# Where a hybrid attention and mLSTM block splits its output weights and squashes its first two gate tiles

## The reference, cut to what matters

```
u    = rmsnorm(x, pre_norm_w)
proj = u @ w_in                                   # 9 groups of 512 columns and 8 gate columns
y_sb = head_rmsnorm(stick_breaking_attention(q, k, v)) * silu(sb_z)      # 8 heads x 64
y_ml = sigmoid(ml_o) * mlstm(conv(q), conv(k), v, i, f)                  # 4 heads x 128
y_ml = head_rmsnorm(y_ml, ml_norm_w) * silu(ml_z)
h    = x + rmsnorm(concat(y_sb, y_ml) @ w_out, post_norm_w)
out  = h + sigmoid(h @ ple_w_gate + b) * (p @ ple_w_up)
```

## Time and profile before

| what | value |
|---|---|
| median of 3 runs | 1822.59 us (1821.94 to 1824.18) |
| the profiled execution | 1821.69 us |
| its span in the trace | 1819.9 us |
| PE busy in the span | 1767.5 us (97%) |
| ACT, DVE, POOL busy | 999.3, 1129.5, 683.6 us |
| end of the attention's last `b_late` | 1257.7 us |
| start of the mLSTM block | 1277.2 us |
| start of the first output projection | 1313.1 us |

### The profile page before, as it was taken

How to read it: one execution, slowest core, us unless ns; L and a number is a source line. 1 busy time by engine, 2 the same in 40 slices (tenths; PEclk the granted TensorE clock), 3 DMA queues, 4 the chain that set the end, 5 groups by cost and what they waited for, 6 DMA issues and landing times. The chain is left out here.

```text
span 1819.9 us, 28179 instructions
## 1 busy us (share of the span) xinstructions
PE 1767.5 (97%) x8972; PEld 1443.2 (79%) x8972; DVE 1129.5 (62%) x1776; ACT 999.3 (55%) x2045; POOL 683.6 (38%) x946
## 2 busy tenths in 40 slices
PE   7999999999899999999999999998799999999998
PEld 6888888878578888888888888886588888788887
DVE  5431214555389888878897898888566666533333
ACT  5431213322277787878777887776777776411111
POOL 2100000000146777777877777765234444200000
PEclk9999999999999999999999999998799999999999
DMA  6677766121494648463745466442465454422220
GB/s 192 164 200 208 231 185 190 46 86 52 130 289 139 179 126 249 131 198 115 234 143 168 147 212 210 145 146 67 133 206 163 161 187 139 164 74 79 81 81 38
DMA packets 193221, 277.05 MB, mean 152 GB/s; under 512 B 66684, under 2 KB 128380, under 8 KB 183896
## 3 DMA queue, kind: packets, MB, share of 16 engines
q1 hardware_dynamic: 189864, 263.10, 47.2%
q0 software_dynamic: 3248, 12.62, 2.0%
HBM read 187.41 MB, written 88.26 MB: 151 GB/s over the span
## 5 line engine op out<-in xcount | busy, mean ns | idle before, releaser
L952 PE MATMUL b_late<-w_split,spare 128*128 128x512 f32 x1536 | 436.7, 412 | 1.0 <-ACT b_p_out L1034 0.6
L732 POOL TENSOR_TENSOR b_a_lo<-b_aT,b_a_hi 128x512 fp32r<-128x512 f32 (+2 forms) x312 | 354.8, 1137 | 25.0
L1104 DVE TENSOR_TENSOR_SCAN b_buf<-b_y,b_buf 128x511 f32<-128x511 f32 (+2 forms) x320 | 357.8, 1118 | 9.2
L505 PE MATMUL a_po<-uT_hi,w_split 128*128 128x512 f32 x1024 | 318.7, 392 | 2.3 <-DVE w_split L387 2.3
L952 PEld LDWEIGHTS b_late<-w_split,spare 128*128 128x128 f32 x1536 | 265.5, 190 | 43.3 <-issue 1.9
L728 POOL CAST b_a_hi<-b_aT 128x512 fp32r<-128x512 f32 (+1 forms) x320 | 182.1, 569 | 199.9 <-PE b_o L926 160.0
L1114 DVE SCALAR_TENSOR_TENSOR b_buf<-b_buf,b_y 128x512 f32<-128x512 f32 (+2 forms) x320 | 189.2, 591 | 104.1 <-PE b_y L912 101.9
L505 PEld LDWEIGHTS a_po<-uT_hi,w_split 128*128 128x128 f32 x1024 | 193.0, 188 | 46.4 <-DVE w_split L387 2.7
L1020 ACT ACTIVATE b_buf<-b_y 128x512 f32<-128x512 f32 (+2 forms) x320 | 171.4, 536 | 76.2 <-PE b_y L906 74.4
L1011 ACT ACTIVATE b_aT<-b_turned 128x512 f32<-128x512 f32 (+1 forms) x320 | 170.6, 533 | 73.8 <-POOL b_a_lo L732 68.7
L505 PE MATMUL a_po<-uT_lo,w_split 128*128 128x512 f32 x512 | 201.6, 394 | 0.0
(11 more groups left out here) (222 smaller groups left out, 3236.1 us busy)
## 6 DMA issues: line engine op xcount, KB each, us to landing
spare<-u_pair SPq DMA_DIRECT2D x64, 1024.0 KB, 5.4
proj_n<-b_p_out SPq DMA_DIRECT2D x64, 256.0 KB, 5.7
c_gates<-proj_n SPq DMA_DIRECT2D x16, 768.0 KB, 4.5
w_raw<-in_w_in POOLq DMA_DIRECT2D x5, 2048.0 KB, 9.8
x_in<-in_x SPq DMA_DIRECT2D x16, 512.0 KB, 4.0
qk_hi<-stage_hi SPq DMA_DIRECT2D x32, 256.0 KB, 2.5
qk_lo<-stage_lo SPq DMA_DIRECT2D x32, 256.0 KB, 2.9
u_pair<-uT_hi SPq DMA_DIRECT2D x16, 512.0 KB, 3.7
```

The costliest lines, as they stand in the source:

```text
L505: mm = pe.matmul(po[t][:], w[:, k, m * P:(m + 1) * P], u[:, k, t * GROUP:(t + 1) * GROUP], start=(k == 0 and n == 0), stop=(k == KT - 1 an ...
L732: nc.gpsimd.tensor_tensor(lo[:, cols], raw, hi[:, cols].bitcast(F32), ALU.subtract).then_inc(lo_done, 1)
L952: mm = pe.matmul(late[:], u_in[f % US][:, u_part, k, :], w[:, k, :], start=(i == 0), stop=(i == PASSES - 1))
L1104: nc.vector.tensor_tensor_scan(down, y[u % YS][:, 1:keys][:, ::-1], down, b[:, keys - 1:keys], ALU.add, ALU.subtract).then_inc(log_done, 1)
```

## The change

Five edits belong together.

1. ACT no longer splits w_out. In the attention's tail POOL makes the high parts of tiles 0 to 3 with a `tensor_scalar` (scale and round), two each at steps 330 and 331, which is behind its last cast. DVE makes their low parts at the same steps, behind the low part of job 319.
2. Tiles 4 to 7 are split in the mLSTM block: POOL makes their high parts as its first four instructions there; DVE makes two low parts in step 0 and two in step 1, each time between its two `numerator` calls. PE waits for all four before the first output projection, and SP before it loads other data into `w_raw` (at step 3).
3. Tiles 4, 5 and 6 get memory of their own, over rows of the gates that are no longer read by then, and are loaded in the middle of the attention, right behind the first two mLSTM tiles' inputs (at about 1104 us). Tile 7 goes where tile 0 was and is loaded at step 331, once the low part of tile 0 is done.
4. ACT squashes the gates of mLSTM tiles 0 and 1 in the attention's tail (`squash_first`, step 329, behind its last exp): sigmoid for both, then silu for both, so with two table loads.
5. In the mLSTM `squash` is left out for tiles 0 and 1.

```diff
+        SPLIT_STEPS, SQUASH_STEP = (UNITS + H_LAG, UNITS + H_LAG + 1), UNITS + X_LAG
+        W_OUT_FIRST = ((0, 1), (2, 3))
...
+            def split_w_out(k):
+                if k == 0:
+                    pool.wait_ge(ml.norm_w_loaded, 32)
+                    pool.wait_ge(late_done, TILES)
+                pool.wait_ge(w_out_loaded[k], 16)
+                nc.gpsimd.tensor_scalar(w_out_hi[:, k, :], w_out_raw[k], ml.norm_w[:, k:k + 1], None, ALU.mult)\
+                    .then_inc(w_out_hi_done, 1)
...
+                    sp.wait_ge(g.pe, 3)
+                    for k in range(4, 7):
+                        sp.wait_ge(w_out_loaded[k % 4], 16)
+                        load_w_out(k)
...
-                for k in range(4, KT):
-                    if n == LATE_STEPS + (k - 4) // 2 + 1:
-                        sp.wait_ge(w_out_lo_done, k - 3)
-                        load_w_out(k)
+                if n == SPLIT_STEPS[1]:
+                    sp.wait_ge(w_out_lo_done, 1)
+                    sp.wait_ge(w_out_loaded[3], 16)
+                    load_w_out(KT - 1)
...
+            def squash_first():
+
+                for c in range(2):
+                    act.wait_ge(ml.gates_loaded[c], 16)
+                    nc.scalar.activation(ml.gates[c][:, 2 * GROUP:], ml.gates[c][:, 2 * GROUP:], ACT.Sigmoid)\
+                        .then_inc(ml.sigmoid_done, 1)
+                for c in range(2):
+                    nc.scalar.activation(ml.gates[c][:, 0:2 * GROUP], ml.gates[c][:, 0:2 * GROUP], ACT.Silu)\
+                        .then_inc(ml.silu_done, 1)
...
+                if isinstance(d, int) and d == 0:
+                    pe.wait_ge(w_out_rest_lo_done, 4)
...
-                    squash(c, s)
+                    if not isinstance(c, int) or c >= 2:
+                        squash(c, s)
...
+            def split_w_out(k):
+
+                raw, hi, _ = ml.w_out_rest[k]
+                pool.wait_ge(ml.w_out_loaded[k], 32)
+                nc.gpsimd.tensor_scalar(hi, raw, ml.norm_w[:, 4 + k:5 + k], None, ALU.mult)\
+                    .then_inc(w_out_rest_hi_done, 1)
+
+            for k in range(4):
+                split_w_out(k)
...
+            def split_w_out(k):
+                raw, hi, lo = ml.w_out_rest[k]
+                dve.wait_ge(w_out_rest_hi_done, k + 1)
+                nc.vector.scalar_tensor_tensor(out=lo, in0=raw, scalar=ml.norm_w[:, 4 + k:5 + k], in1=hi.bitcast(F32),
+                                               op0=ALU.mult, op1=ALU.subtract).then_inc(w_out_rest_lo_done, 1)
...
+                if isinstance(c, int) and c < 2:
+                    split_w_out(2 * c)
+                    split_w_out(2 * c + 1)
```

More of the change, by code:

```diff
@@ L661, in attention_and_projection @@
         late_stored = [sem(f"late_stored{s}") for s in range(2)]
-        w_out_loaded = [sem(f"w_out_loaded{n}") for n in range(4)]
+        w_out_loaded = ml.w_out_loaded
         w_out_hi_done = sem("w_out_hi_done")
@@ L665, in attention_and_projection @@
         raw = w_raw[:].rearrange("p k n -> p (k n)").rearrange("p (k n) -> p k n", n=D_MODEL)
-        w_out_raw = [raw[:, k % 4, :] for k in range(KT)]
         def load_q(sp, n):
@@ L690, in attention_and_projection @@
         R = H * TOK
+        with nc.sbuf_tensor("w_out_over_gate_rows", [P, 3 * D_MODEL], F32) as over_gate_rows:
+            pass
         g = GateRows(nc, ctx)
@@ L694, in flat @@
             return t[:].rearrange("a h c -> a (h c)")
+        w_out_raw = [raw[:, k, :] for k in range(4)] + \
+            [over_gate_rows[:, k * D_MODEL:(k + 1) * D_MODEL] for k in range(3)] + [raw[:, 0, :]]
+        ml.w_out_rest = [(w_out_raw[k], w_out_hi[:, k, :], w_out_lo[:, k, :]) for k in range(4, KT)]
         y = [psum(f"b_y{s}", [P, GROUP]) for s in range(YS)]
@@ L761, in _ @@
                     split(n - H_LAG)
+                if n in SPLIT_STEPS:
+                    for k in W_OUT_FIRST[SPLIT_STEPS.index(n)]:
+                        split_w_out(k)
         @block.sync
@@ L1088, in _ @@
                 gates_exp(n)
-                for k in range(KT):
-                    if n == LATE_STEPS + k // 2:
-                        split_w_out(k)
+                if n == SQUASH_STEP:
+                    squash_first()
         @block.vector
@@ L1312, in __init__ @@
             for name in ("c_qk_loaded", "c_v_loaded", "c_gates_loaded"))
+        self.w_out_loaded = [ctx.enter_context(nc.semaphore(f"w_out_loaded{n}")) for n in range(4)]
+        self.sigmoid_done = ctx.enter_context(nc.semaphore("c_sigmoid_done"))
+        self.silu_done = ctx.enter_context(nc.semaphore("c_silu_done"))
 class GateRows:
@@ L1389, in mlstm_and_output_projection @@
         post_w_loaded = sem("c_post_w_loaded")
+        w_out_rest_hi_done = sem("c_w_out_rest_hi_done")
+        w_out_rest_lo_done = sem("c_w_out_rest_lo_done")
         y_in = [sb(f"c_y_in{s}", [P, SB_WIDTH]) for s in range(2)]
@@ L1411, in mlstm_and_output_projection @@
         y_loaded, x_loaded = map(per_slot, ("c_y_loaded", "c_x_loaded"))
-        sigmoid_done = sem("c_sigmoid_done")
-        silu_done = sem("c_silu_done")
+        sigmoid_done, silu_done = ml.sigmoid_done, ml.silu_done
         scores_done = sem("scores_done")
@@ L1494, in step @@
                 if isinstance(c, int) and c == LAG:
+                    sp.wait_ge(w_out_rest_lo_done, 4)
                     prefetch(range(4))
```

6 lines of the change are left out of this document (removed).

## The result

| | before | after |
|---|---|---|
| median (20 runs each) | 1822.22 us | 1824.96 us |
| ratio, 95% interval | | 1.0016 (1.001 to 1.0022) |
| profiled execution: span | 1819.9 us | 1825.1 us |
| last copy of `b_late` to the block's start (tail) | 19.3 us | 21.1 us |
| block's start to the first `c_out` (ramp) | 35.9 us | 38.3 us |

The account below looks back on a forecast made before the run. PE was taken as the bound from 1313.1 on, so the first output projection's shift moves the end: tail -2.0 and ramp +1.4 gave -0.6 us, 1822.0 us by the median, range 1818.2 to 1826.5.

Parts of the forecast that it names:

- What bounds each stretch: Tail: DVE late next, by 2.8 us, once PE's and ACT's waits go; ramp: a chain over ACT to DVE.
- the tail: Attention's end: last sum starts at 1272.0 instead of 1274.0, so the mLSTM block starts 2.0 us earlier.
- without a gap: Attention's tail: DVE busy from about 1262 to the sum at 1272, 9.2 us of work including POOL's exclusion.
- POOL's price: POOL's new 128x1024 instruction: 1.1 us each, about 0.95 of it keeping DVE out; upper end 2.41.
- They add up instead of overlapping: Tail: w_out's low parts on DVE and POOL's new instructions exclude each other; four of POOL add 3.8 us.
- The ramp: mLSTM's start to first c_out: +0.9 and +0.5 for the clock, in all +1.4 us.
- Step 0: mLSTM ramp: second numerator starts 10.75 us behind the block's start instead of 11.86, 1.1 earlier.
- The two low parts of step 1: mLSTM ramp: they add 2.5 us on DVE; less 1.1 and 0.5, the step comes out 0.9 later.
- the second scores of step 2: mLSTM ramp: PE's scores run at the clock's lower level, 1.22 us against 0.71, costing +0.5.
- case D: POOL's instruction costs between 1.6 and 2.1 us: time 1825 to 1826; chance 0.09.
- Rival C: POOL's instruction costs 2.4 us: tail 3.3 later, ramp +2.9, together +6.2, time 1828.8; chance 0.13.
- the main case: Whole kernel: 0.6 us faster, 1822.0, spanning 1820.5 to 1824.5 with POOL's price up to 1.6; chance 0.58.

Follow-up runs that it names:

- e3: Changed kernel without DVE's four low parts of tiles 4 to 7 in mLSTM steps 0 and 1: 1821.19 us, ratio 0.9997 to before.
- e5: Kernel before with only the gates' part (squash of tiles 0 and 1 in the tail, behind ACT's last copy): 1820.21 us, ratio 0.9988 to before.
- e8: e7 with the squash of tiles 0 and 1 back in the mLSTM's steps 0 and 1: ratio 0.9995 to before.
- e1: Changed kernel with POOL's eight new instructions as casts only, without scaling by the norm weights: 1820.69 us, ratio 0.9995 to before.
- e9: e7 with POOL's four tail scalings as tensor_scalar again, the mLSTM's two staying tensor_tensor: ratio 0.9969 to before.
- e6: e2 with POOL's eight scalings as tensor_tensor with the weight's column broadcast: 1821.19 us, ratio 0.9994 to before.
- e7: Changed kernel rearranged: high parts on ACT and POOL (tensor_tensor), low parts mostly behind the last sum, squash behind ACT's last copy: 1816.96 us, ratio 0.9976 to before.
- e4: Changed kernel with POOL's four ramp instructions in four forms (constant tensor_scalar, tensor_tensor, cast, two tensor_scalar halves): one execution, ramp 36.2 us.
- e2: Changed kernel with DVE's four tail low parts behind the attention's last sum and tile 7 loaded later: 1823.25 us, ratio 1.0005 to before.

## Why the prediction was wrong

- **What bounds each stretch: right for the ramp, half right for the tail.** PE's waits in the tail went, the last sum stood behind DVE's low parts instead of ACT's copy, the squash and then DVE bound the ramp (e3, e5, e8), and the block's start followed the last sum by 3.17 us (1276.85 to 1280.03, that is 3.18). ACT's copy was forecast 9.5 us behind the last copy of `b_late`, and came at 9.5. But DVE was to be at work "without a gap", kept late by taking turns with POOL; in fact it stood idle for 5.0 us in four waits, and POOL's own row held it: 11.84 us, 0.1 to the last low part, and 1.2 for that one, are the 13.15 from 1263.70 to the sum at 1276.85. The prediction counted POOL's instructions only as time taken from DVE, which at 1.1 us an instruction could not show.
- **POOL's price: this step failed.** I took 1.1 us from the casts, "since it too reads one tile and writes the same type", and 2.41 as the upper end. It costs 2.84, more than that end: an operation with a second tile was no bound for an operation of another kind. e1, with the price that I took, gives -1.9 by the two lengths against -0.6 forecast; in time it has 0.9995, not told from 1, where after has 1.0016. So it is the mis-sized term that turned the sign of the two lengths (+4.1 against -1.9).
- **"They add up instead of overlapping": right for the casts and the two-input form, too strict for `tensor_scalar`.** A low part that started while POOL's instruction of 2.84 us was under way lost 0.8 us (2.06 against 1.28), in a row of them 0.4 each while POOL's lost 0.47 each (e9). Rival C, with 2.4 us an instruction in full exclusion, had +3.3 in the tail and +2.9 in the ramp; the dearer price with the milder exclusion gave +1.8 and +2.35. The Trainium skill has the second one to issue block fully (SBUF — State Buffer, Summary: rules for kernel authors). e6's and e7's rows agree (2.37 instead of 0.69 beside an operation of 1.90), the rows of `tensor_scalar` do not, and the measurement decides.
- **The ramp: +1.4 forecast, +2.35 measured, +0.9 in e1.** Step 0 gained nothing instead of 1.1 (the second `numerator` 11.8 behind the block's start, against 11.9), since POOL was at work until 11.3 and not 4.6. The two low parts of step 1 made the next tile's products 1.7 late (27.9 against 26.1), and the second scores of step 2 at the lower level of the clock (1.22 us against 0.71) cost the rest, 0.6, as forecast. In e1 the second scores of step 1 ran at the upper level (0.71), in after at the lower (1.22), so a part of the 1.5 us between their ramps is the clock's.
- **The chances.** The measured time is that of case D (1825 to 1826, chance 0.09), with a price above that of C (0.13); that the time still lies in the range is luck, since C's own sum at 2.84 would come out above its 1828.8, and only the milder exclusion kept the time below. Two bounds do not follow from the prediction's own terms: the main case reaches down to 1821.5 by them and not 1820.5 (only the clock's 0.5 is taken off), and D, from 1.6 us an instruction on, begins at 1824.0 (-2.0 + 2.0 + 1.4) and not at 1825. The main case had 0.58 on a price for which no row of the trace stood; the upper side of it should have had more weight and reached past the nearest row.
- **Medians and profiles.** The two stretches give +4.1, the ratio +2.9 with an interval of 1.8 to 4.0. In e5 they give -3.5 against -2.2 by the ratio, in e9 -5.8 against -5.6. A profiled execution carries the steps of the clock outside the two lengths, 1.5 to 1.6 us each. That they are what parts the lengths from the ratios is not shown; one profile of each kernel doesn't tell.

## What to carry to other kernels

A price read from the nearest operation is no bound for one of another kind: if an instruction has no row in the trace, measure it alone before moving work to it, and put the instruction that ends a block ahead of work that merely has to be done by then. When one engine's work is moved, count what the receiving engine already does in that stretch: ACT lost 10.5 us of work in the ramp here, and the ramp grew. An engine's gaps of 2.5 us between two instructions that wait for another engine (DVE in step 0) took three low parts for 0.6 us of ramp (31.8 in e7, 31.2 in e5), although beside POOL they took 2.96, 2.57 and 1.27. With that, the last sum ahead of most of the split, and two high parts back on ACT, the same work that cost 4.1 us in the changed kernel gained 5.1 to 5.8 by the two lengths.

## What the runs showed of the hardware

- GpSimd, one operation of 128x1024 to the type for TensorE: cast 1.04 us, `tensor_tensor` with a broadcast column 1.90, `tensor_scalar` 2.77 with a constant and 2.84 with a pointer (e4, after). The Trainium skill (GPSIMD Engine Reference, Engine selection) calls one input roughly line rate. Against DVE's 1.24 for a low part of as many columns, the cast (1.04) agrees and `tensor_scalar` does not.
- What it does to DVE depends on the operation. DVE's low part (two SBUF inputs, 1.24 in a row) took 2.87 beside the `tensor_tensor` (e7). Beside the `tensor_scalar` it took 2.06 when it started in the middle of one (after) and 1.63 in a row (e9). Beside the casts the mean of four is 1.80 (e1), but the casts were done 2.3 us before the last of the four ended. So the slower form gave the shorter tail (17.4 in e9 against 18.4 in e7).
- PE's granted clock differs between profiles where the instructions are the same: over the same 5 us, in which PE was busy throughout, it was 0.68 with 17 matmuls in before and 1.00 with 23 in e2.
